# Moving the activations by 64 bytes in SBUF, and requesting six conditioning blocks one unit earlier, in a two-layer decoder step

## The reference

```python
mod = silu(c) @ w_ada[i] + b_ada[i]          # c: one vector for the prompt, one for each of the 8 sequences
sh1, sc1, g1, sh2, sc2, g2 = split(mod, 6)
h = x * (1 + sc1) + sh1
z = h @ w_in[i]                              # q, k, v (8 heads x 64) and the two halves of the conv input
o = dilated window attention(q, k, v)        # prompt, or new tokens against a cache of 512
cz = silu(layernorm(depthwise_conv(glu)))    # width 31
mix = concat(rms(o) * beta_a, rms(cz) * beta_c) @ w_out[i]
x = layernorm(alpha * x + g1 * mix)
h = x * (1 + sc2) + sh2
x = layernorm(alpha * x + g2 * ((silu(h @ w_gate[i]) * (h @ w_up[i])) @ w_down[i]))
```

## The kernel before, in words

| tensors | start, modulo 128 |
|---|---|
| x, w_raw, w_hi, w_lo, eye, ones | 0 |
| rope, mp, msc, msn, h_mul | 0 |
| h_add, b_ada, pend, c_in, small | 32 |
| mod / vec | 64 / 96 |
| ring, cache_a, cache_b, mean_h, sq_h, acc_h, h, big | 0 |
| qk, vT, vnat, sqc, uP, a_hi, a_lo, gate, af, sq_x, mean_x, rows, Os, PTs | 0 |
| uS, y, oT, rowsc, rstdc, zcos, zraw, taps, E, PT, mt, gm, Qz, Es, hf, acc_x | 96 |

## Time and profile before

### The profile page before, as it was taken

One profiled execution on the slowest core, in us unless ns is written; L12 is line 12 of the kernel. 1 busy time (PEld: TensorE's weight loads), 2 busy tenths in 40 slices (PEclk: granted clock), 3 DMA queues, 4 the chain that ended last, 5 costly groups with the idle time before them and its releaser, 6 DMA issues.

```text
span 1582.8 us, 26321 instructions
## 1 busy us (share of the span) xinstructions
PE 1500.7 (95%) x11456; PEld 1359.0 (86%) x11456; DVE 766.4 (48%) x1207; ACT 548.7 (35%) x862; POOL 84.9 (5%) x104
## 2 busy tenths in 40 slices
PE   5999988889999999999989999889899999999996
PEld 2887766779999999899979977569799999999995
DVE  1798974364232232322347989846633333332233
ACT  3425566134222222211235255662533222221122
POOL 1000000111000000001001000002100000000100
PEclk7999999989999999999999999989899999999998
DMA  9576244623334433332214542514022222222221
GB/s 382 179 170 175 94 188 173 261 79 147 137 143 160 160 149 143 134 112 78 80 56 133 80 123 98 225 78 140 29 92 81 80 81 88 86 77 84 77 71 61
DMA packets 59523, 197.16 MB, mean 125 GB/s; under 512 B 22544, under 2 KB 22928, under 8 KB 48400
## 3 DMA queue, kind: packets, MB, share of 16 engines
q1 hardware_dynamic: 59408, 195.48, 37.1%
HBM read 187.27 MB, written 8.18 MB: 123 GB/s over the span
## 4 chain that ended last, share of the span: by engine, by line
PE 83%; DVE 6%; ACT 5%; DMA 2%; issue 2%; SPq 0%; POOL 0%; ACTq 0%; DVEq 0%; POOLq 0%
PE ps L1231 68%; PE ps L1340 2%; PE ps L1251 2%; PE ps L1609 2%; DVE sb_y L875 2%; DMA sb_x<-xT 1%; PE ps L1373 1%; ACT sb_E L589 1%; PE ps L1260 1%; PE ps L1281 1%; PE ps L1484 1%; DVE sb_h L858 1%; PE ps L1407 1%; DMA sb_ring<-w_ada 1%; PE ps L1396 1%
## 5 line engine op out<-in xcount | busy, mean ns | idle before, releaser
L1231 PE MATMUL ps<-sb_h,sb_w_hi 128*128 128x288 f32 x4224 | 770.2, 299 | 0.0
L1231 PEld LDWEIGHTS ps<-sb_h,sb_w_hi 128*128 128x128 f32 x4224 | 627.5, 189 | 51.8 <-issue 50.8
L1231 PE MATMUL ps<-sb_h,sb_w_lo 128*128 128x288 f32 x2112 | 451.8, 296 | 0.0
L839 DVE TENSOR_TENSOR sb_w_lo<-sb_w_raw,sb_w_hi 128x1024 fp32r<-128x1024 f32 x192 | 234.8, 1224 | 357.5 <-ACT sb_w_hi L508 357.1
L1231 PEld LDWEIGHTS ps<-sb_h,sb_w_lo 128*128 128x128 f32 x2112 | 340.1, 189 | 0.0
L508 ACT ACTIVATE sb_w_hi<-sb_w_raw 128x1024 fp32r<-128x1024 f32 x192 | 202.1, 1053 | 320.1 <-PE ps L1231 305.8
L875 DVE SCALAR_TENSOR_TENSOR sb_y<-sb_uP,sb_vec,sb_y 128x512 f32<-128x512 f32 x240 | 164.9, 744 | 0.5
L1231 PE MATMUL ps<-sb_a_hi,sb_w_hi 128*128 128x288 f32 x704 | 151.8, 297 | 0.0
L1231 PE MATMUL ps<-sb_a_lo,sb_w_hi 128*128 128x288 f32 x704 | 150.8, 296 | 0.0
L1231 PE MATMUL ps<-sb_a_hi,sb_w_lo 128*128 128x288 f32 x704 | 150.7, 296 | 0.0
L803 ACT ACTIVATE sb_a_hi<-sb_af 128x576 fp32r<-128x576 f32 x44 | 30.2, 686 | 266.7 <-DVE sb_af L1185 266.7
(11 more groups left out here) (192 smaller groups left out, 1208.6 us busy)
## 6 DMA issues: line engine op xcount, KB each, us to landing
sb_w_raw<-w_mix SPq DMA_DIRECT2D x144, 512.0 KB, 3.5
sb_ring<-w_ada SPq DMA_DIRECT2D x40, 1024.0 KB, 5.8
sb_w_raw<-w_dn SPq DMA_DIRECT2D x32, 512.0 KB, 3.5
sb_ring<-vc_d SPq DMA_DIRECT2D x12, 1024.0 KB, 8.5
sb_big<-w_ada SPq DMA_DIRECT2D x8, 1024.0 KB, 11.9
sb_ring<-kc_d SPq DMA_DIRECT2D x8, 1024.0 KB, 7.5
sb_w_raw<-w_dn SPq DMA_DIRECT2D x16, 384.0 KB, 3.2
sb_cache_a<-kc_d SPq DMA_DIRECT2D x4, 1024.0 KB, 7.4
```

Source lines behind the costliest of these rows:

```text
L839: nc.vector.tensor_tensor(w_lo[:, g % NW, :], w_raw[:, g % NR, :], w_hi[:, g % NW, :].bitcast(F32), ALU.subtract)\
L1231: ins = nc.tensor.matmul(z[:, i], a[:, g % NW, w], b[:, k0 + k, i * H:(i + 1) * H], start=first and k == 0 and t == 0, stop=last and k == ...
```

## The change

A tensor `gap` of 16 float32 (64 bytes in each partition) is allocated after `ones` and used by nothing. Everything allocated after it moves up by 64 bytes: what started at 0 modulo 128 starts at 64, what started at 32 at 96, what started at 96 at 32. x, w_raw, w_hi, w_lo, eye and ones stay where they are. The end of the layout moves from byte 229248 to byte 229312.

In `around`, the quads 18 to 23 are issued at unit `at + 2` instead of `at + 3`; the quads 16 and 17 were at `at + 2` already.

```diff
         eye = sb("eye", [P, P])
         ones = sb("ones", [P, P])
+        sb("gap", [P, 16])
         rope = sb("rope", [P, 2, T])
...
                 if l == 0:
                     for n, (at, _) in OUT_QUADS.items():
-                        if u == at + (2 if n < 18 else 3):
+                        if u == at + 2:
                             if n < 18:
                                 sp.wait_ge(s["os_ps"], nth(0, "os_ps", 2))
                             fetch_quad(n)
```

## The result

The changed kernel takes 1576.73 us (median of 6 runs, 1573.41 to 1581.25), the kernel before 1584.09 us in the same comparison. The ratio is 0.9958, 95% interval 0.9946 to 0.9971: 0.42% faster. The profiled execution of the changed kernel took 1580.11 us, 3.4 us over its median, with a span of 1578.3 us; beside the one of before (1584.71) it shows only 4.6 us of gain.

What follows compares the result with a forecast made beforehand. TensorE was taken as the bound, busy 95% of the span, with 8448 matmuls at 133.2 ns and a few stalls. 1584.7 - 4.3 (requests) + 0 (gap) = 1580.4, forecast as 1580.5 us, range 1573 to 1589.

Steps and rivals of the forecast that it cites:

- I take 1 us from the issue to the first bytes: Quad 20's landing in layer 0's output projection: 1 us plus 12.1 us of bytes from 290.3, landing at about 303.4.
- Part 1: Earlier quad requests, layer 0's output projection: old stall's 5.7 us go, new one costs 1.1 + 0.3; sum -4.3 us.
- rival A: Layer 0's quads: the stall only moves, to quad 20, clock falling behind it; 1583.6 us, up to 1588; chance 0.15.
- by it I take 0 for the fp32r products too: TensorE's fp32r products (L1231): new starts change nothing, 0 us, inferred from a float32 product's equal times.
- rows 10: Profile rows of L1289, float32 product of 288 columns, moving operand at 96 or 0 modulo 128: median 406 ns both.
- part 2: The gap's shift of starts, for VectorE, ScalarE, TensorE and transfers: claimed 0 us; bounds for TensorE -103 to +113 us.
- The hint of 0 and 128 modulo 256: fp32r products: row halves start alternately at 0 and 128 modulo 256, and 133.2 ns hold for both alike.
- rival B: fp32r products of L1231: the gap frees TensorE, 32 to 103 us faster, time 1477 to 1549; chance 0.08.
- small effects of the gap: Whole kernel: the gap changes the time by under 2%, of either sign; chance 0.08.
- 10.7 ns x 8448: L1231's matmuls: 10.7 ns over the skill page's 122.5 ns each; if the gap gave all back, an estimated 1495 us.
- Rival C: fp32r products of L1231: start at 64 costs a tenth 128-byte piece, 13.4 ns each, 113 us, time 1694; chance 0.06.
- Rival D: Layer 0's quad requests: transfers don't keep queue order, quad 18's 4.1 us stall stays, 1584.7 us; chance 0.05.

Runs made afterwards that it cites:

- e2_again: One traced execution of the kernel before with only the earlier quad requests, no gap; that kernel measured 1583.06 us (12 runs), ratio 1.0002.
- g96: Kernel before with a gap of 96 bytes, requests as before, so activations start at 96 and weights at 0 modulo 128; 1584.69 us, ratio 1.0027.

## Why the prediction was right, and where it wasn't

**Requests, step by step.** Right: quad 18 is requested at 285.6 (285.8 forecast), lands in 5.3 us and waits no more; its stall had cost 5.7 us; the stores go out at 290.4 and 291.9 (290.7 and 291.1 forecast), the weight block behind them at 292.4 (292); quad 20 is what is late next; no later unit waits for its weights. Wrong: quad 20's landing, 306.8 instead of 303.4. With it the new stall was 4.8 us of idle time instead of 1.1, and 7.1 us with the slower clock instead of 1.4. The bytes (4.98 MB) and the rate were right: from quad 19's landing to quad 20's, 3.93 MB took 9.3 us, which is 422 GB/s. The step that failed is "I take 1 us from the issue to the first bytes", with the reason that most of the 3 us of way "overlaps other transfers". Taken from the measured times the way is 306.8 - 290.3 - 12.1 = 4.4 us, and it doesn't overlap. It is there for the first of the series already: quad 19 was to land at 290.3 + 1 + 2.5 = 293.8 by the same sum and landed at 297.5, and the block of unit 26, forecast at 301, landed at 304.3. A part of it is the start (0.2 MB in the first 2 us, which is why the first row shows 264 GB/s), the rest is the 2.5 us and more between the bulk of the bytes and the landing; the lone quad 18 had its bytes moved by 290.0 and landed at 290.9. That one DMA engine lags behind the rest in a filled queue would explain it and is not shown. The quad and the block requested after quad 20 took nothing from it that the landings show: they landed behind it, each by its own bytes' time. Part 1 was worth +1.4 us by the two stalls (7.1 - 5.7; +0.6 with the 6.3 of e2_again) and nothing that the times can tell (1.0002), where I had -4.3. This is rival A, "the stall only moves", which had 0.15; it allowed for up to 1588 us without the gap, and 1584.7 + 1.4 lies within that.

**Gap, step by step.** VectorE, ScalarE and the transfers: nothing, as forecast. TensorE: 0 forecast, measured 1.11 ns a matmul, 9.4 us over all 8448, of which 7.7 us show in the medians of the gap alone. The step that failed is "by it I take 0 for the fp32r products too", with rows 10 as the nearest row. The prediction had named this risk (float32 runs at half the pace) and took 0 all the same. The row was blind in two ways. Its two operands started 96 and 0 bytes from their weights (`ones`, at 0), and by g96 such a pair shows nothing even at full pace. And when they start 32 and 64 apart, as in the changed kernel, they are still the same twice (404 ns), so float32 at half the pace doesn't show what fp32r shows. By the prediction's own sign, a pace that differs by more than 0.5 ns, part 2 was wrong. The hint of 0 and 128 modulo 256 was right for what it says and just as blind. It was rival B in mechanism, at 9 us and not at the 32 to 103 that B needed to stand apart; "small effects of the gap" had 0.08. Two of the recorded sums are slips that nothing hangs on: the price of B worked out in full is 1580.4 - 103 = 1477, not 1480, and 10.7 ns x 8448 off 1584.7 are 1494, not 1495.

**Why the number held.** It held by luck. The forecast was 0.27% and the measurement 0.42%, by two errors that nearly cancel: 5.7 us too much for the requests, 8 to 9 too little for the gap. The measured 1576.73 us lies just below the 1577 to 1583 that the forecast itself had at 0.58. The range held because its lower end, 1573, left room for half of the small effects of the gap. Rival C is excluded: 10 pieces for 9 would have cost 13.4 ns. Rival D, transfers that don't keep their order, didn't come: quad 18 landed first, and the seven behind it landed in the order of the requests.

The Trainium skill (SBUF — State Buffer, Specifications (TRN2)) counts cachelines of 16 bytes, by which a start at 64 is like a start at 0; the runs disagree for TensorE's pace, where 64 and 0 differ by 1.11 ns a matmul and 32 and 0 by nothing. The same page says in its section "Who interferes with whom" that TensorE's two read ports, for weights and for the moving operand, are independent; that the pace hangs on where these two stand to each other speaks against full independence in this kernel, though no run shows that the ports are the place.

## What to carry to other kernels

Where fp32r products set the end, try weights and activations 64 bytes apart modulo 128, high and low parts of the weights at the same start: a spare tensor of 64 bytes gave 0.8% of the pace here, and the longest uninterrupted stretch of the chain shows it to 0.01 ns when run times still wander by 5 us and more. Before a request is put forward in a queue, list what it pushes behind it, and look for an empty stretch for the transfers that nobody waits for: the stall behind the two stores cost 5.7 us in one order of the quads and 7.1 in the other by the traces, and none when the stores went out 32 to 41 us earlier. When a landing time is forecast, add the way in full to the bytes' time: 2.8 us for the lone quad here, 4.4 us behind the filled queue. A row is near to a question only if the two cases that it compares differ in the thing asked.

## What the runs showed of the hardware that wasn't expected

- TensorE's pace with fp32r operands of 288 columns depends on the start of the moving operand against the stationary one modulo 128: 133.33 ns at 0, 32 and 96 apart, 132.22 ns at 64, 132.78 and 133.89 ns with the high and low weights at different starts. The four lie 0.55 ns apart, in equal steps.
- In a filled queue the landings lag the bytes: seven requests landed in the order in which they were issued, 1.3 to 3.2 us apart, and the last at 310.5, when all but 0.03 MB of the seven had been moved by 308.0. The lone quad ahead of them landed within 1.5 us of its last bytes. Quad 20 took 12.4 us, where what was left at its request, itself included, makes 9.5 us at 412 GB/s.
- A stall costs TensorE more than its length, and not in proportion: 1.6 us behind 4.12 us of idle time (before), 1.6 behind 3.51 (gap alone), 2.3 behind 4.77 (changed kernel), 2.7 behind 3.58 (requests alone). In the changed kernel the granted clock is at its lower level (0.50, 1.2 GHz) from us 305 to 311.
